# Asking for the compression weights and the second input from ScalarE's queue

## The chip, the cores and the metric

One NeuronCore of one Trainium2 chip runs the whole program. The metric is the device time of one execution in microseconds (us).

## The reference

All arrays are float32; the input x has 256 tokens of width 1024. Two blocks follow each other. The first has two layers (DEPTH = 2), and the change lies in them:

```python
for i in range(DEPTH):
    h = rmsnorm(x, norm_mix[i])
    z = h @ w_in[i]                       # 1024 x 5400
    (q_a, kc, vc, ks_, vs_, kw, vw, g_nsa, rq, rk, rv, rg, merge_a, merge_b) = split_cols(z, IN_SPLITS)
    y_a = nsa_mixer(q_a, kc, vc, ...) @ w_up_nsa[i]
    y_b = retention(rq, rk, rv, rg) @ w_up_ret[i]
    x = x + (sigmoid(merge_a) * y_a + sigmoid(merge_b) * y_b) @ w_out[i]
    x = x + square(relu(rmsnorm(x, norm_mlp[i]) @ w_ff1[i])) @ w_ff2[i]
    gate = sigmoid(rmsnorm(x, norm_ple[i]) @ w_ple_gate[i])
    x = x + gate * (p[i] @ w_ple[i])
```

Inside the mixer, the columns kc and vc of z are compressed: overlapping windows of 32 tokens (plus a learned position term) go through `gelu(zb @ w1) @ w2`, with w1 of 2048 x 256 and w2 of 256 x 64 for keys and the same for values. These are the arrays cmp_w1_k, cmp_w1_v, cmp_w2_k and cmp_w2_v. The array p (2 x 256 x 256) is the second input; it is used only at the end of a layer. The second block (a stick-breaking attention with a state-space model, a sparse attention, two MLPs) is untouched by the change.

## The kernel before

Every large matrix is multiplied in two-digit form: ScalarE copies a weight tile to a rounded high part (`act_split`, line 1053, two halves of 128 x 2048 each), VectorE or GpSimd subtracts it to get the low part (`lower_half`, line 1073, written over the tile in the ring), and TensorE makes three matmuls for each product (line 463).

**The ring.** The weight tiles, 2 MB each (128 x 4096 floats), pass through three SBUF buffers (`RING = 3`). The order is `TILES`: in0 to in10 (512 columns of w_in each), then up_nsa, up_ret, out0, out1, the MLP's and the gate's tiles. Tile n lies in buffer n % 3. SyncE's program (lines 2970 to 3018) walks through TILES, waits until TensorE has used up the tile three places earlier (`tile_used`, line 2998), and issues the tile's load (line 3016). So in4 needs in1's buffer, and in5 needs in2's. SyncE's queue runs in order: whatever it issues between two tiles stands ahead of the second.

**The compression's weights.** Just ahead of in4 (`n == RING + 1`, line 2988), SyncE issues five loads of cmp_w1 (`W1_PARTS`, line 2991: 13 and 3 blocks of the key's matrix, 10, 4 and 2 blocks of the value's; a block is 128 rows of 256 floats, moved in runs of 1 KB; together 4 MB), then the two w2 (line 2994, 64 KB each, runs of 256 bytes) and p (line 2995, 256 KB, runs of 1 KB). They signal `w1_in` (5 x 16) and `late_in` (3 x 16). The parts lie in columns of z that chunks 4 to 10 write later, and in parts of the buffer `work`.

**TensorE in the stretch.** Chunk c computes the 512 columns of tile in{c}, token half 0 and then token half 1 (c{c}t0, c{c}t1), 24 matmuls each, into two PSUM banks used in turn (`wide`). So c2t0 needs the bank of c1t0, and c3t1 the bank of c2t1, to be saved by ScalarE first. After chunk 2 stand four transposes of kc and vc, then chunk 3, then a wait on `w1_in` (line 805) and the compression's matmuls, then transposes that wait for the normalised queries and keys.

**ScalarE in the stretch.** The order is written out by hand in `act_layer`. `save_half(c, t)` (line 1153) copies a bank to z; `act_split` waits for the tile and for the place of its high part:

```python
for c in range(3):
    save_half(c, 0)
    act_split(st, act, TILES, SPLITS, f"in{c + 2}")
    save_half(c, 1)
act.wait_ge(st.last.sem, st.reached())
act.activation(sq, z[:, :, 0:1152], ACT.Square)...
```

So c2t1 is saved only behind in4's split, and the squares of the norm (line 1186) follow it; VectorE then sums them (line 1427), ScalarE takes the root, and VectorE multiplies queries and keys (line 1342). The places of the high parts matter: in3's (`tmp`, `rows`) are in1's, the second of in4's (`work`) is in2's. GpSimd makes the low parts of the in tiles.

Of the kernel before, what the change touches and what calls it, by code (L numbers as in the profile page):

```python
# [14 lines left out]
P = 128  # L15
# [9 lines left out]
RING = 3  # L25
# [5 lines left out]
NCMP, CMP_STRIDE, CMP_LEN, CMP_HID = 16, 16, 32, 256  # L31
# [242 lines left out]
def program(nc, ctx, I, out):  # L274
    address = {}

    def sb(name, shape):
        address[name] = -(-nc.sbuf_base // 32) * 32
        return ctx.enter_context(nc.sbuf_tensor(name, shape, F32))
# [5 lines left out]
    def sig(name, per_layer=0, start=0):  # L285
        return Signal(ctx.enter_context(nc.semaphore(name)), per_layer, start)
# [12 lines left out]
    p_sb = sb("p_sb", [P, TT, PLE])  # L299
# [35 lines left out]
    def part(lo, width, pattern=None, **sizes):  # L335
        ap = work[:, lo:lo + width]
        return ap.rearrange(pattern, **sizes) if pattern else ap
# [9 lines left out]
    W1_PARTS = [(0, 0, 13, z[:, 0, W1_Z:W1_Z + 13 * CMP_HID]), (0, 13, 3, z[:, 1, W1_Z:W1_Z + 3 * CMP_HID]),  # L347
                (1, 0, 10, z[:, 1, W1_Z + 3 * CMP_HID:W1_Z + 13 * CMP_HID]), (1, 10, 4, part(4032, 4 * CMP_HID)),
                (1, 14, 2, part(7264, 2 * CMP_HID))]
# [37 lines left out]
    late_in = sig("late_in", 16 * 3)  # L387
    w1_in, ple_in = sig("w1_in", 16 * len(W1_PARTS)), sig("ple_in", 16)
# [42 lines left out]
    def batch_heads(b):  # L431

        _, h0, nh = BATCHES[b]
        return [4 * g + h for g in range(GROUPS) for h in range(h0, h0 + nh)]
# [10 lines left out]
    def w_tile(n, shape):  # L445

        k, m = shape
        return ring[n % RING][:, 0:k * m].rearrange("p (k n) -> p k n", k=k)
# [583 lines left out]
    def act_norm(st, act, signal=None, power=-0.5, squares=gate_t):  # L1032


        for t in range(TT):
            act.activation(squares[:, t, :], x[:, t, :], ACT.Square, accum_out=nss[:, t:t + 1]).then_inc(st.up(act_step), 1)
        act.wait_ge(st.last.sem, st.reached())
        act_rsqrt(st, act, nrr, nss, 1.0 / D, EPS, signal, power)

    def act_split(st, act, tiles, splits, name, halves=(0, 1)):  # L1040

        n = tiles.index(name)
        act.wait_ge(tile_in[n % RING].sem, st.at(tile_in[n % RING], 16 * (n // RING + 1)))
        places, width = PLACES if splits is SPLITS else PLACES2, split_halves(name)
        for h in halves:

            place = places[name][h]
            earlier = [tiles.index(o) for o in splits[:splits.index(name)] if place in places[o]]
            before = [TILES.index(o) - len(TILES) for o in SPLITS if place in PLACES[o]]
            n_used = (before + earlier)[-1] + 1 + RING if before + earlier else 0  # L1050
            if n_used > 0:
                act.wait_ge(tile_used.sem, st.at(tile_used, n_used))
            act.activation(w_hi[place][:, 0:width], ring[n % RING][:, h * width:(h + 1) * width], ACT.Copy) \  # L1053
                .then_inc(st.up(w_hi_ready), 1)
# [90 lines left out]
    def act_layer(act, st, following):  # L1145
        wide_, aux_ = wide.again(WIDE), aux.again(AUX)

        def save_half(c, t):

            m = min(BANK, D_IN - c * BANK)  # L1150
            b, nth = wide_.next(f"c{c}t{t}")
            act.wait_ge(wide_.ready.sem, st.at(wide_.ready, nth))
            act.activation(z[:, t, c * BANK:c * BANK + m], b[:, 0:m], ACT.Copy, scale=nrr[:, t:t + 1]).then_inc(st.up(wide_.saved), 1)
# [18 lines left out]
        if st.where.layer == 0:  # L1172
            act_norm(st, act)
            act_split(st, act, TILES, SPLITS, "in0")
            act_split(st, act, TILES, SPLITS, "in1")
        else:
            act_split(st, act, TILES, SPLITS, "in1")
            act.wait_ge(ple_added.sem, st.at(ple_added, 0))
            act_norm(st, act)
            act.wait_ge(st.last.sem, st.reached())  # L1180
        for c in range(3):
            save_half(c, 0)
            act_split(st, act, TILES, SPLITS, f"in{c + 2}")
            save_half(c, 1)
        act.wait_ge(st.last.sem, st.reached())
        act.activation(sq, z[:, :, 0:1152], ACT.Square).then_inc(st.up(sq_ready), 1)
        act.wait_ge(ss_ready.sem, st.at(ss_ready, 1))
# [14 lines left out]
        kv, nth = aux_.banks[aux_.names.index("w2") % 2], aux_.names.index("w2") + 1  # L1202
# [19 lines left out]
        b, nth = wide_.next("o0")  # L1222
# [19 lines left out]
        b, nth = wide_.next("o1")  # L1242
# [24 lines left out]
        for n in range(4):  # L1267
            t, half = divmod(n, 2)
# [11 lines left out]
        for n in range(4):  # L1280
            c, t = divmod(n, 2)
            b, nth = wide_.next(f"g{n}")
# [1670 lines left out]
    def small_loads(i):  # L2953

        def vec(name):
            return I[name][i:i + 1]

        small = [(vec_rows[8 * n:8 * n + 8, :], vec(v).rearrange("o (k p) -> (o k) p", p=P))
                 for n, v in enumerate(("norm_mix", "norm_mlp", "norm_ple"))]
        for n, v in ((C_Q, "nsa_q_norm"), (C_K, "nsa_k_norm")):  # L2960
            for u in range(2):
                small.append((vec_rows[n:n + 1, u * DH:(u + 1) * DH], vec(v)))
        for n, v in enumerate(("cmp_pos_k", "cmp_pos_v")):
            small.append((vec_rows[C_POS + 16 * n:C_POS + 16 * n + 16, :],
                          I[v][i].rearrange("(j l) d -> j (l d)", l=2)))
        for n, v in enumerate(("cmp_w2_k", "cmp_w2_v")):
            small.append((w2[:, n], I[v][i].rearrange("(h p) d -> p h d", p=P)))
        return small

    @block.sync  # L2970
    def _(sp):
        sp.dma_start(x[:, :, :], I["x"][0].rearrange("(t p) n -> p t n", p=P)).then_inc(x_in.sem, 16)
        for i in range(DEPTH):
            where = Where(i)

            def src(name):
                return I[name][i]

            if i:
                sp.wait_ge(small_used.sem, i * small_used.per_layer + 1)  # L2980
            small = small_loads(i)
            if i:
                for n, (dst, s) in enumerate(small[:9]):
                    sp.dma_start(dst, s).then_inc((small_in if n else mix_in).sem, 16)
            for n, name in enumerate(TILES):
                if n == RING and i == 0:
                    sp.dma_start(const[:, P:CONST_W], I["const"][:, P:CONST_W]).then_inc(const_in.sem, 16)
                if n == RING + 1:
                    for kind, j0, nj, place in W1_PARTS:
                        s = src("cmp_w1_" + "kv"[kind])[j0 * P:(j0 + nj) * P, :]  # L2990
                        sp.dma_start(place.rearrange("p (j n) -> p j n", n=CMP_HID),  # L2991
                                     s.rearrange("(j p) n -> p j n", p=P)).then_inc(w1_in.sem, 16)
                    for dst, s in small[9:]:
                        sp.dma_start(dst, s).then_inc(late_in.sem, 16)
                    sp.dma_start(p_sb[:, :, :], I["p"][i].rearrange("b s n -> (b s) n")
                                 .rearrange("(t p) n -> p t n", p=P)).then_inc(late_in.sem, 16)

                sp.wait_ge(tile_used.sem, where.value(tile_used, n + 1))
                if name == "ff1.3":
                    sp.dma_start(w_ple, src("w_ple").rearrange("(k p) n -> p k n", p=P)).then_inc(ple_in.sem, 16)  # L3000
                kind, _, num = name.partition(".")
                if name.startswith("in"):
                    c = int(name[2:])
                    m = min(BANK, D_IN - c * BANK)
                    s, k = src("w_in")[:, c * BANK:c * BANK + m], KT
                elif name in ("up_nsa", "up_ret"):
                    s, k, m = src("w_" + name), 4, D
                elif kind == "ff1":
                    s, k, m = src("w_ff1")[:, int(num) * BANK:(int(num) + 1) * BANK], KT, BANK
                elif kind == "ff2":  # L3010
                    s, k, m = src("w_ff2")[int(num) * BANK:(int(num) + 1) * BANK, :], 4, D
                else:
                    c = int(name[-1])
                    s = src("w_out" if name.startswith("out") else "w_ple_gate")[:, c * BANK:(c + 1) * BANK]
                    k, m = KT, BANK
                sp.dma_start(w_tile(n, (k, m)), s.rearrange("(k p) n -> p k n", p=P)) \
                    .then_inc(tile_in[n % RING].sem, 16)
        sp_tail(sp)
# [77 lines left out]
```

## Time and profile before

| | |
|---|---|
| median of 3 runs | 1503.27 us (1499.74 to 1503.67) |
| profiled execution | 1503.03 us, its span 1501.2 us |
| TensorE busy (PE) | 1448.0 us, 96% of the span |
| weight loads (PEld) | 1236.6 us, 82% |
| VectorE (DVE) | 814.0 us, 54% |
| ScalarE (ACT) | 729.6 us, 49% |
| GpSimd (POOL) | 289.2 us, 19% |
| mean granted TensorE clock | 0.993 of full speed |
| DMA | 250.25 MB, mean 167 GB/s |

The engines run side by side, so busy times don't add up. The chain that ended last is followed back from the last instruction to what released each step; its shares tell where the time is set. SPq is SyncE's sequencer with its DMA issues, ACTq is ScalarE's. A DMA issue has a duration of its own, in which the sequencer can do nothing else, and a time to landing. Times in rows are us from the start of the span, unless they are marked as ns. L3016 is line 3016 of the kernel.

### The profile page before, as it was taken

How to read it: one execution, taken by the hardware profiler on the slowest of the kernel's cores; microseconds unless marked ns; L12 is line 12 of the kernel's file. 1: busy time of each engine (PE TensorE's matmuls, PEld its weight loads, DVE VectorE, ACT ScalarE, POOL GpSimd, SP SyncE). 2: the span in 40 equal slices, each digit the busy share in tenths (PEclk: the TensorE clock that was granted, in tenths of full speed). 3: DMA queues.
4: the chain of work that ended last, by engine and by line, in shares of the span. 5: the costliest groups of instructions: out<-in, count | busy, mean ns of one | idle time of the engine just before them, and what ended most of it. 6: DMA issues, size and time to landing. Idle time of an engine off the chain costs nothing.

```text
span 1501.2 us, 19974 instructions
## 1 busy us (share of the span) xinstructions
PE 1448.0 (96%) x8638; PEld 1236.6 (82%) x8638; DVE 814.0 (54%) x1010; ACT 729.6 (49%) x909; POOL 289.2 (19%) x109
## 2 busy tenths in 40 slices
PE   7899999999999999999999989899999999999998
PEld 5688888989877688889989778587988888889986
DVE  5337664444552355754444659876444557654445
ACT  4364635445444563645445346655454326265452
POOL 4589140000027695410000000000000004000000
PEclk9999999999999999999999999999999999999999
DMA  8732435645538432446545362315555453156451
GB/s 309 254 135 89 166 114 200 221 170 200 191 125 302 144 122 98 165 157 230 186 174 205 75 228 99 140 38 187 197 203 189 145 197 113 41 198 236 170 184 69
DMA packets 123142, 250.25 MB, mean 167 GB/s; under 512 B 16960, under 2 KB 28976, under 8 KB 122928
## 3 DMA queue, kind: packets, MB, share of 16 engines
q1 hardware_dynamic: 122792, 248.89, 47.0%
q8 instruction: 68, 1.11, 0.3%
q14 instruction: 18, 0.15, 0.0%
q10 hardware_dynamic: 264, 0.10, 0.0%
HBM read 247.93 MB, written 1.05 MB: 166 GB/s over the span
## 4 chain that ended last, share of the span: by engine, by line
PE 82%; DVE 8%; SPq 5%; DMA 3%; ACT 2%; issue 1%; DVEq 0%; ACTq 0%
PE psum L463 79%; PE psum L470 3%; SPq L2991 2%; DMA ring<-in_w_in 1%; SPq L1817 1%; DVE scr L2499 1%; DVE big L2499 1%; SPq L1810 1%; DMA ring<-in_sb_ssm_w_in 1%; DVE x L2505 1%; DMA ring<-in_w_ff 1%; DVE p_sb L2499 0%; DVE w_lo L1073 0%; DVE rows L2499 0%; DMA work<-in_norm_mix 0%
## 5 line engine op out<-in xcount | busy, mean ns | idle before, releaser
L463 PE MATMUL psum<-ht_hi,w_lo 128*128 128x256 f32 x960 | 270.3, 282 | 7.3 <-issue 3.1
L463 PE MATMUL psum<-w_lo,ht_hi 128*128 128x512 f32 (+1 forms) x576 | 226.0, 392 | 0.0
L463 PE MATMUL psum<-w_lo,hid_hi 128*128 128x512 f32 x512 | 202.4, 395 | 0.0
L463 PEld LDWEIGHTS psum<-ht_hi,w_lo 128*128 128x128 f32 x960 | 180.4, 188 | 10.0 <-issue 8.9
L1053 ACT ACTIVATE w_hi_work<-ring 128x2048 fp32r<-128x2048 f32 x41 | 78.4, 1911 | 150.3 <-PE psum L463 148.8
L1073 DVE TENSOR_TENSOR w_lo<-ring,w_hi_work 128x2048 fp32r<-128x2048 f32 x29 | 66.5, 2292 | 127.2 <-ACT w_hi_work L1053 127.2
L1143 DVE TENSOR_TENSOR hid_lo<-work,hid_hi 128x512 fp32r<-128x512 f32 x60 | 41.5, 692 | 161.9 <-ACT hid_hi L1121 161.9
L463 PEld LDWEIGHTS psum<-w_lo,ht_hi 128*128 128x128 f32 x576 | 109.9, 191 | 21.2 <-issue 1.0
L463 PE MATMUL psum<-ht_lo,w_hi_tmp 128*128 128x256 f32 x448 | 125.6, 280 | 0.0
L463 PE MATMUL psum<-ht_hi,w_hi_tmp 128*128 128x256 f32 x448 | 125.4, 280 | 0.0
L463 PE MATMUL psum<-ht_lo,w_hi_rows 128*128 128x256 f32 x448 | 125.0, 279 | 0.0
L463 PE MATMUL psum<-ht_hi,w_hi_rows 128*128 128x256 f32 x448 | 124.4, 278 | 0.0
L463 PEld LDWEIGHTS psum<-w_lo,hid_hi 128*128 128x128 f32 x512 | 96.1, 188 | 21.7
L1073 DVE TENSOR_TENSOR w_lo<-ring,w_hi_tmp 128x2048 fp32r<-128x2048 f32 x36 | 82.5, 2293 | 46.8 <-ACT w_hi_tmp L1053 46.8
L1073 POOL TENSOR_TENSOR w_lo<-ring,w_hi_work 128x2048 fp32r<-128x2048 f32 x12 | 57.3, 4779 | 260.5 <-ACT w_hi_work L1053 260.5
L1117 ACT ACTIVATE work<-psum 128x512 f32<-128x512 f32 x60 | 35.8, 597 | 144.1 <-PE psum L463 144.1
L463 PE MATMUL psum<-hT,ring 128*128 128x256 f32 (+2 forms) x480 | 91.2, 350 | 6.2 <-DMA ring<-in_sb_ssm_w_in 4.7
L463 PEld LDWEIGHTS psum<-hT,ring 128*128 128x128 f32 (+1 forms) x480 | 79.4, 189 | 17.0 <-issue 7.8
L463 PE MATMUL psum<-w_hi_big,hid_lo 128*128 128x512 f32 x224 | 88.9, 397 | 0.0
L463 PE MATMUL psum<-w_hi_big,hid_hi 128*128 128x512 f32 x224 | 88.4, 395 | 0.0
L463 PE MATMUL psum<-w_hi_work,hid_hi 128*128 128x512 f32 x224 | 88.4, 395 | 0.0
L1053 ACT ACTIVATE w_hi_tmp<-ring 128x2048 fp32r<-128x2048 f32 x42 | 80.0, 1905 | 17.1 <-PE psum L463 10.4
(395 smaller groups left out, 3396.9 us busy)
## 6 DMA issues: line engine op xcount, KB each, us to landing
ring<-in_w_ff SPq DMA_DIRECT2D x32, 2048.0 KB, 7.9
ring<-in_mlp_w SPq DMA_DIRECT2D x32, 2048.0 KB, 8.5
ring<-in_w_in SPq DMA_DIRECT2D x20, 2048.0 KB, 8.4
ring<-in_w_out SPq DMA_DIRECT2D x4, 2048.0 KB, 8.2
ring<-in_w_ple_gate SPq DMA_DIRECT2D x4, 2048.0 KB, 8.0
ring<-in_sb_ssm_w_in SPq DMA_DIRECT2D x4, 2048.0 KB, 10.8
ring<-in_dsa_w_in SPq DMA_DIRECT2D x3, 2048.0 KB, 8.5
ring<-in_w_up_nsa SPq DMA_DIRECT2D x2, 2048.0 KB, 8.5
```

Source lines behind the costliest of these rows:

```text
L463: ins = pe.matmul(o, lhsT, rhs, start=start, stop=stop)
L470: ins = pe.transpose(o, in_, ident[0:n, 0:n])
L1053: act.activation(w_hi[place][:, 0:width], ring[n % RING][:, h * width:(h + 1) * width], ACT.Copy) \
L1073: eng.tensor_tensor(w_lo[n % RING][:, c], ring[n % RING][:, c], w_hi[places[name][h]][:, 0:width].bitcast(F32), ALU.subtract) \
L1117: act.activation(h, b, ACT.Relu).then_inc(st.up(wide_.saved), 1)
L1143: dve.tensor_tensor(lo, h, hi.bitcast(F32), ALU.subtract).then_inc(st.up(hid_lo_ready), 1)
L1810: sp.dma_start(dst, src).then_inc(signal.sem, 16)
L1817: sp.dma_start(dst, src, allow_slow_non_contiguous=True).then_inc(signal.sem, 16)
L2499: return dve.tensor_tensor(o, a, b, op)
L2505: return dve.scalar_tensor_tensor(out=o, in0=a, scalar=s1, in1=b, op0=op0, op1=op1)
L2991: sp.dma_start(place.rearrange("p (j n) -> p j n", n=CMP_HID), s.rearrange("(j p) n -> p j n", p=P)).then_inc(w1_in.sem, 16)
```

## The change

The eight loads leave SyncE's program and are issued by ScalarE, in both layers, behind the save of c0t1 (the end of the first turn of the loop above). Data, destinations and signals stay the same.

```diff
+        def load_compression():
+            i = st.where.layer
+            for kind, j0, nj, place in W1_PARTS:
+                s = I["cmp_w1_" + "kv"[kind]][i][j0 * P:(j0 + nj) * P, :]
+                act.dma_start(place.rearrange("p (j n) -> p j n", n=CMP_HID),
+                              s.rearrange("(j p) n -> p j n", p=P)).then_inc(w1_in.sem, 16)
+            for dst, s in small_loads(i)[9:]:
+                act.dma_start(dst, s).then_inc(late_in.sem, 16)
+            act.dma_start(p_sb[:, :, :], I["p"][i].rearrange("b s n -> (b s) n")
+                          .rearrange("(t p) n -> p t n", p=P)).then_inc(late_in.sem, 16)
+
         for c in range(3):
             save_half(c, 0)
             act_split(st, act, TILES, SPLITS, f"in{c + 2}")
             save_half(c, 1)
+            if c == 0:
+                load_compression()
...
                     sp.dma_start(const[:, P:CONST_W], I["const"][:, P:CONST_W]).then_inc(const_in.sem, 16)
-                if n == RING + 1:
-                    for kind, j0, nj, place in W1_PARTS:
-                        s = src("cmp_w1_" + "kv"[kind])[j0 * P:(j0 + nj) * P, :]
-                        sp.dma_start(place.rearrange("p (j n) -> p j n", n=CMP_HID),
-                                     s.rearrange("(j p) n -> p j n", p=P)).then_inc(w1_in.sem, 16)
-                    for dst, s in small[9:]:
-                        sp.dma_start(dst, s).then_inc(late_in.sem, 16)
-                    sp.dma_start(p_sb[:, :, :], I["p"][i].rearrange("b s n -> (b s) n")
-                                 .rearrange("(t p) n -> p t n", p=P)).then_inc(late_in.sem, 16)
```

## Rows read from the trace of the kernel before

**Rows 1.** The page: TensorE's share of the span, and the chain by engine.
```profile
PE 1448.0 (96%) x8638; PEld 1236.6 (82%) x8638; DVE 814.0 (54%) x1010; ACT 729.6 (49%) x909; POOL 289.2 (19%) x109
...
PE 82%; DVE 8%; SPq 5%; DMA 3%; ACT 2%; issue 1%; DVEq 0%; ACTq 0%
```
**Rows 2.** The chain in order of time, layer 0: start us, us, what.
```profile
29.05 0.37 SPq L3016
...
29.46 0.58 SPq L2991
...
30.08 6.20 SPq L2991
...
42.23 1.42 SPq L2991
...
45.16 0.71 SPq L2995
...
45.91 11.12 DMA ring<-in_w_in
...
60.77 0.58 ACT big L1153
...
75.45 30.01 PE psum L463 x159
```
**Rows 3.** TensorE's timeline: start, us; in brackets idle before and its releaser.
```profile
39.82 0.39 PE L463 MATMUL psum<-w_hi_work,ht_lo 128*128 128x512 f32 x1
...
61.40 0.79 PE L463 MATMUL psum<-w_hi_tmp,ht_lo 128*128 128x512 f32 x1 [4.24 <-ACT big L1153]
...
61.99 0.63 PE L463 MATMUL psum<-w_lo,ht_hi 128*128 128x512 f32 x1
...
69.61 3.00 PE L463 MATMUL psum<-big,work 128*32 128x256 f32 x50
...
471.33 0.39 PE L463 MATMUL psum<-w_hi_work,ht_lo 128*128 128x512 f32 x1
...
491.97 0.50 PE L463 MATMUL psum<-w_hi_tmp,ht_lo 128*128 128x512 f32 x1 [3.30 <-ACT big L1153]
...
499.31 3.00 PE L463 MATMUL psum<-big,work 128*32 128x256 f32 x50
```
**Rows 4.** Windows: length, PE, PEld, DVE, ACT, POOL busy; PEclk, DMA share, GB/s.
```profile
61.40:65.00 3.60, 3.60 (x9) 2.83 (x10) 1.46 (x1) 2.10 (x1) 3.60 (x2) 0.50 0.01 3
```
**Rows 5.** The chain in order of time, layer 1.
```profile
460.79 5.39 SPq L2991
...
476.62 10.98 DMA ring<-in_w_in
```
**Rows 6.** ScalarE's timeline in both layers: saves of c0t1, in3's split.
```profile
32.74 0.66 ACT L1153 ACTIVATE big<-psum,tiny 128x512 f32<-128x512 f32 x1
...
40.31 1.92 ACT L1053 ACTIVATE w_hi_tmp<-ring 128x2048 fp32r<-128x2048 f32 x1 [5.20 <-PE psum L463]
...
463.72 0.67 ACT L1153 ACTIVATE big<-psum,tiny 128x512 f32<-128x512 f32 x1
...
471.82 1.92 ACT L1053 ACTIVATE w_hi_tmp<-ring 128x2048 fp32r<-128x2048 f32 x1 [5.20 <-PE psum L463]
```
**Rows 7.** ScalarE's longest DMA issue at the start: ns min/median/max.
```profile
L3039 ACTq DMA_DIRECT2D work<-in_norm_mix x1: 540/540/540, 1.3 to 1.3; - x1
```
**Rows 8.** Queue's packets, MB, share, in windows 29.05:36.29, 29.05:45.87, 36:37, 51:53.
```profile
q1 hardware_dynamic: 1129, 2.17, 85.4%
...
q1 hardware_dynamic: 4423, 5.52, 99.2%
...
q1 hardware_dynamic: 342, 0.36, 108.9%
...
q1 hardware_dynamic: 378, 0.77, 105.0%
```
**Rows 9.** The same in layer 1, windows 459.75:466.18 and 459.75:473.92.
```profile
q1 hardware_dynamic: 928, 1.90, 83.9%
...
q1 hardware_dynamic: 3515, 4.60, 97.3%
```
**Rows 10.** VectorE's timeline, layer 0: the last of the norm's multiplications.
```profile
69.23 0.75 DVE L1342 TENSOR_TENSOR big<-big,tiny 128x256 f32<-128x256 f32 x2
```

## The prediction

> **What bounds the kernel now.** I read the page first, then the chain that ended last in order of time, then the instruction timelines of SyncE, ScalarE and TensorE around the added and removed lines, then the count of packets that the DMA queue moved. TensorE is busy 96% of the span and the chain lies on it for 82%, but 5% of the chain is SyncE's queue [rows 1]: that is where this change acts, once in each layer. The chain shows the place [rows 2]. SyncE asks for in3 at 29.05, and then spends from 29.46 to 45.87 issuing the five compression parts, the two w2 and p. Only then is in4 asked for, and it lands 11.12 us later, at 57.03. ScalarE has been standing before in4's split; it splits (two halves) and only then saves c2t1 at 60.77. TensorE needs that bank for the second half of chunk 3 and has been idle for 4.24 us [rows 3]. Its clock pays as well: from 61.40 to 65.00 the granted clock is 0.50, the lower of the two levels (1.2 of 2.4 GHz), after the idle stretch, and a matmul lasts 0.63 us against 0.39 [rows 3, 4].
>
> The size of the loss, from the starts of the matmuls [rows 3]: chunk 2 starts at 39.82 and runs gapless with chunk 3's first token to 61.40 - 4.24 = 57.16, so 17.34 us for three halves of 24 matmuls and four short transposes, 5.66 us a half. The last half should end 23.0 us after chunk 2's start; the compression's matmuls start at 69.61, 29.8 us after it. So 6.8 us are lost in layer 0: 4.24 idle and 8.21 - 5.66 = 2.55 for the low clock. In layer 1, 499.31 - 471.33 = 28.0, so 5.0 lost, 3.30 of it idle. The most that the change can give is 11.8 us. The layer 1 issues look the same as in layer 0 [rows 5].
>
> **The change, part by part.** (a) SyncE loses eight issues in each layer, 16.4 us of its queue's time. What keeps in4 back is then its slot: in1 must be used. ScalarE's split of in3 at 40.31 waits for the same event [rows 6], so in4 is asked for at about 40.3 instead of 45.91, and in layer 1 at 471.8 instead of 476.62 (5.6 and 4.8 us earlier, no more).
>
> (b) The eight issues now stand in ScalarE's own stream, behind the save of c0t1, which ends at 33.40 and 464.39 [rows 6]. The question is how long they hold ScalarE. Its nine small issues at the start took at most 0.54 us each [rows 7]; on SyncE the unhindered ones took 0.58 and the others 1.4 to 6.2 [rows 2]. Packet counts explain them [rows 8]. in3 is 1024 packets of 2 KB, the five parts are 1664, 384, 1280, 512 and 256 packets of 1 KB, each w2 is 256. When the last of the eight issues ended (45.87), SyncE had earlier given the queue 5632 packets (through the second w2) and 4423 were moved: 1209 outstanding. In layer 1 the issue of the fifth part ended when 4864 had been given and 3515 moved: 1349 [rows 9]. An issue thus ends when all before it is down to some 1200 to 1350 packets; the first reading of layer 1, 2688 given and 928 moved, would allow 1760 [rows 9]. I assume the same depth for ScalarE's queue, which no row shows.
>
> So ScalarE is free when 4608 - 1209 = 3400 of its packets are moved (layer 1: 4608 - 1349 = 3260). Rates: 342 packets of 1 KB per us, 378/2 = 189 of 2 KB [rows 8]. in3's packets end near 36.0 (1129 moved at 36.29, 105 of them beyond in3), and they began 1.5 us after its issue (1024/189 = 5.4 back from 36.0). Until 36.0 the sharing with in3 only swaps one for the other; from then the parts flow alone until in4's first packets at 40.3 + 1.5 = 41.8: 5.8 x 342 = 1980 moved, 1420 to go. Both loads then share the DMA engines, which one queue alone already fills (108.9% and 105.0%) [rows 8]. How they share, no row shows. With no share for in4: 4.2 us, free at 46.0. By equal bytes: 1420/342 + 710/189 = 7.9, free at 49.7. By equal packets: 1024 pairs take 8.4, the other 396 take 1.2, free at 51.4. I take equal bytes, the middle one. Layer 1: in3's packets end at 466.7, in4's start at 473.3, 2257 moved, 1002 to go; free at 476.2, 478.9 or 481.5.
>
> The Trainium skill, DMA: Bandwidth & Descriptors, section Queues, rings and completion order, says that each DMA engine takes turns between queues by whole packets of descriptors; if these hold equally many descriptors for both loads, that is the third value, and the sum would be +16.4 us. No run here shows two big queues side by side.
>
> (c) What is queued behind ScalarE's issues: the save of c1t0, the split of in3, the save of c1t1. TensorE ends chunk 1 at 39.82 and 471.33 [rows 3] and needs c1t0's bank at once. It therefore stands from 39.82 to 49.7 + 0.69 (one save) = 50.4, where now it stands 4.24 us later on. Then chunk 2 and 3 take their 23.0 us and the low clock its 2.55 once more (the larger of the two layers' values, since this idle is longer). The other work keeps up: in4 has landed by then, the split of in3 (3.8 us) and c1t1's save are done 5 us into chunk 2, c2t1 is saved about 3 us after chunk 2's end, some 3 us before chunk 3's second half. The norm chain, which ends with VectorE's multiplications 9.2 us after c2t1's save (60.77 to 69.98) [rows 2, 10], is done before the compression's matmuls end. in5 and in6 are asked for later, by the same amount as TensorE. The compression weights have landed before 56, some 20 us before they are used. All this costs nothing while that holds; without that cover the first thing late would be the norm chain, by 1 to 3 us.
>
> (d) The sum. The compression's matmuls start at free + 0.69 + 23.0 + 2.55 = free + 26.2. Layer 0: 75.9 against 69.61, +6.3. Layer 1: 505.1 against 499.31, +5.8. TensorE is gapless for 30 us from 75.45 on [rows 2], so the delay reaches the end. Total +12.1 us on an execution of 1503.03 us (span 1501.2), whose time is 0.2 below the median of the runs, too little to correct: **1515.1 us**. Bounds: no share for in4 and 1760 outstanding give free at 44.3 and 475.0, +0.9 and +1.9, total +2.8, 1506; equal packets give +8.0 and +8.4, total +16.4, 1519.5.
>
> **Rivals.**
> Faster: ScalarE's queue takes the eight without blocking, 0.62 us each as the first one on SyncE, and is free at 38.4, before TensorE needs c1t0. in4 shares with the parts from 41.8, at worst 8.4 us, lands near 52, and c2t1 is saved before 57.2. The whole 6.8 + 5.0 = 11.8 us come back: 1491.3. For it: the part's bytes are few and ScalarE's queue is empty. Against it: every run of such issues on SyncE blocked as soon as a thousand packets were ahead [rows 2, 5]. Chance 0.12.
> The Trainium skill, same page, section Issuing engines are not separate DMA queues, says that issuing from several engines saves the sequencer's issue time, which is usually small beside the DMA; by that rule this rival wins. The trace disagrees for this load: the issues took 16.4 us.
>
> About the same: the queue holds more than SyncE's seemed to, or the descriptors of in4 are made only after those of the parts, so that ScalarE is free near 44. The break-even is free = 43.4 and 473.1. It gives 1503 to 1508, and in it one wait of 4 us is swapped for another. For it: layer 1's first reading. Against it: the last reading of each layer, 1209 and 1349. Chance 0.10.
>
> The forecast, ScalarE blocked to about 50 and 479: chance 0.78, of which 0.05 lies above 1521 (in3's split or the norm chain late as well). That the change does nothing is excluded but for the small gain in (a).
>
> **Numbers.** 0.3% is 4.5 us, about what a measurement of this kernel can tell from no change. Faster 0.12, within 0.10, slower 0.78. The range must leave out at most 0.2: the faster case and the uppermost tail, so it runs from 1503 to 1521. The forecast's own range is 1506 to 1520.
>
> **What would show it.** In the profile after: the eight issues on ScalarE's queue, ending near 50 and 479, the middle ones 2 to 6 us long; TensorE idle about 10 and 7.5 us at the start of chunk 2, released by ScalarE's save; no wait before chunk 3's second half; in4 asked for near 40.3; the granted clock at 0.5 behind the new idle. Eight short issues would make me wrong, and so would an end of ScalarE's issues before 44: then the depth or the sharing of the queues was misread. If the issues end where I say and the time still does not grow, the step (d) is wrong.

## The result, and the profile after

The changed kernel takes 1507.56 us (median of 13 runs, 1504.64 to 1509.01) against 1503.27 us (1499.74 to 1504.95, 13 runs): ratio 1.0029, interval 1.0021 to 1.0036, so 3.2 to 5.4 us more. Two later measurements gave 1.0022 (1.0011 to 1.0033) and 1.0035 (1.0015 to 1.0054). The profiled execution took 1504.64 us, span 1502.8, the fastest of the 13; executions of one kernel differ by 4 to 5 us, so below I compare stretches of a few tens of us and not whole spans.

The page of the changed kernel: the shares, SyncE's queue gone down on the chain from 5% to 2%, and a second queue (q10, ScalarE's) that now moves 9.27 MB (0.10 before).

```profile
PE 1447.0 (96%) x8638; PEld 1235.5 (82%) x8638; DVE 812.3 (54%) x1010; ACT 729.8 (49%) x909; POOL 289.3 (19%) x109
...
q10 hardware_dynamic: 10248, 9.27, 2.0%
...
PE 85%; DVE 8%; SPq 2%; issue 2%; DMA 1%; ACT 1%; POOL 1%; DVEq 0%; ACTq 0%
```

ScalarE's timeline in layer 0, changed kernel (start, us; idle before in brackets). It answers to [rows 2, 6].

```profile
29.61 4.94 ACTq L1185 DMA_DIRECT2D big<-in_cmp_w_k  x2
...
33.17 0.66 ACT L1153 ACTIVATE big<-psum,tiny 128x512 f32<-128x512 f32 x1
34.58 2.91 ACTq L1185 DMA_DIRECT2D big<-in_cmp_w_v  x1
37.52 5.95 ACTq L1185 DMA_DIRECT2D work<-in_cmp_w_v  x2
43.50 0.60 ACTq L1188 DMA_DIRECT2D work<-in_cmp_w_k  x1
44.12 1.17 ACTq L1188 DMA_DIRECT2D work<-in_cmp_w_v  x1
45.33 0.72 ACTq L1189 DMA_DIRECT2D p_sb<-in_p  x1
46.10 0.69 ACT L1153 ACTIVATE big<-psum,tiny 128x512 f32<-128x512 f32 x1 [12.27 <-issue]
```

Two things are to be seen. The issues do hold ScalarE: the save of c1t0, whose bank was full by about 34.4 in the kernel before, is made at 46.10. And they begin at 29.61, though the save of c0t1, which stands ahead of them in the program, runs only at 33.17: the sequencer passed the copies on to the engine and went ahead to the next issue, since every wait that stands between was met by then. The depth of the queue can be read too. When the last issue ended (46.05, and 475.01 in layer 1), ScalarE had earlier given its queue 4608 packets, and 3273 and 2965 of them were moved (windows 29:46.05 and 459:475.01): 1335 and 1643 outstanding, where the prediction took 1209 and 1349 from SyncE's queue.

TensorE's timeline, both layers, changed kernel, which answers to [rows 3]:

```profile
46.88 0.77 PE L463 MATMUL psum<-w_hi_work,ht_lo 128*128 128x512 f32 x1 [6.47 <-issue]
...
71.57 3.00 PE L463 MATMUL psum<-big,work 128*32 128x256 f32 x50
...
475.85 0.77 PE L463 MATMUL psum<-w_hi_work,ht_lo 128*128 128x512 f32 x1 [4.69 <-issue]
...
501.06 3.00 PE L463 MATMUL psum<-big,work 128*32 128x256 f32 x50
```

The wait has changed places: 4.24 us before chunk 3's second half are gone, and 6.47 us stand before chunk 2; in layer 1 it is 3.30 against 4.69. From the end of chunk 1 to the compression's matmuls it was 69.61 - 39.82 = 29.79 and 27.98 us; it is 71.57 - 40.41 = 31.16 and 501.06 - 471.16 = 29.90. That is 1.4 and 1.9 us more, 3.3 together, the lower end of what the runs show. (I count from chunk 1's end because the two traces also drift by some 2 us between the two layers.) The clock pays in the new place as it did in the old one. Windows of the changed kernel (length, PE, PEld, DVE, ACT, POOL busy, granted clock, DMA share, GB/s), the first the idle stretch, the second the first nine matmuls behind it:

```profile
40.41:46.88 6.47, 0.00 (x1) 0.03 (x1) 0.00 (x0) 0.69 (x1) 0.29 (x1) 0.77 1.09 348
...
46.88:50.80 3.92, 3.92 (x9) 3.12 (x10) 0.00 (x0) 3.05 (x2) 1.06 (x1) 0.51 1.12 336
```

Last, in4's load. It should have been asked for at 40.3; SyncE asked at 47.68 (changed kernel, SyncE's timeline), and ScalarE's split of in4, which waits for its landing, starts at 56.99, where it started at 57.06 before. TensorE now needs what hangs on it later, so no second wait arises:

```profile
47.68 0.37 SPq L3020 DMA_DIRECT2D ring<-in_w_in  x1
...
56.99 1.92 ACT L1053 ACTIVATE w_hi_hT<-ring 128x2048 fp32r<-128x2048 f32 x1 [1.81 <-DMA ring<-in_w_in]
```

The program says why. A used tile is not given back by its own last matmul (that one signals the full bank) but by the next instruction of TensorE that has no signal of its own (`pay` in `mm`, called by `tile_done`'s debt). Behind chunk 1 that is chunk 2's first matmul, and this one waits for ScalarE's save of c1t0. So ScalarE's block held back in4's request too.

### The profile page after: what moved, and what is told of

Same layout as the page of the kernel before. It is cut to its first block, busy times and chain, and to the rows that moved or that the text cites. A ratio compares the mean times of both kernels' runs of the same rounds, so it can differ in the third digit from the quotient of the medians.

```text
span 1502.8 us, 19974 instructions
## 1 busy us (share of the span) xinstructions
PE 1447.0 (96%) x8638; PEld 1235.5 (82%) x8638; DVE 812.3 (54%) x1010; ACT 729.8 (49%) x909; POOL 289.3 (19%) x109
## 3 DMA queue, kind: packets, MB, share of 16 engines
q10 hardware_dynamic: 10248, 9.27, 2.0%
## 4 chain that ended last, share of the span: by engine, by line
PE 85%; DVE 8%; SPq 2%; issue 2%; DMA 1%; ACT 1%; POOL 1%; DVEq 0%; ACTq 0%
PE psum L463 82%; PE psum L470 3%; SPq L1830 1%; DVE scr L2512 1%; DVE big L2512 1%; SPq L1823 1%; DMA ring<-in_sb_ssm_w_in 1%; DVE x L2518 1%; POOL w_lo L1073 1%; DVE p_sb L2512 0%; DVE rows L2512 0%; DMA work<-in_norm_mix 0%; DVE rows L1355 0%; DVE pT L2762 0%; DVE p_sb L2518 0%
## 5 line engine op out<-in xcount | busy, mean ns | idle before, releaser
L463 PE MATMUL psum<-w_hi_work,hid_lo 128*128 128x512 f32 x224 | 88.2, 394 | 0.0
## 6 DMA issues: line engine op xcount, KB each, us to landing
ring<-in_sb_ssm_w_in SPq DMA_DIRECT2D x4, 2048.0 KB, 11.3
```

The costliest lines, as they stand in the source:

```text
L463: ins = pe.matmul(o, lhsT, rhs, start=start, stop=stop)
```

## The experiments

Two theories stood after this. A: ScalarE's blocked issues stall TensorE, and the stall holds back in4; the block's length is the bytes that in3 and the parts have to move. B: something of the queues themselves (the order in which the hardware takes them, or the traffic) sets the time, whoever issues. Each expectation below puts its own A and B, narrowed to what the run can tell apart. The edits of the runs from e5_release to e3_three are shown against the changed kernel, that of e4_sp_behind against the kernel before.

**in1 given back early (e5_release).** The changed kernel and one instruction more on TensorE:

```diff
         for c in range(1, 3):
             chunk(c)
+            if c == 1:
+                tp(scores[:, 3 * BANK:3 * BANK + P], ident)
```

> The changed kernel, with one transpose of the identity (into an unused PSUM bank) behind chunk 1, so that in1 is given back by it and no longer by chunk 2's first matmul. Theory A (in4 came late in the changed kernel because in1's release hangs on a matmul that itself waits for ScalarE; the two queues share by equal packets, 122 against 122 per us while in3 and the parts overlapped): in4 is asked for near 40.5 and 471.3, its packets start 1.5 us later beside the parts, ScalarE's last issue ends near 51.5 instead of 46.05 and near 478.8 instead of 475.01, TensorE starts chunk 2 5.4 and 3.8 us later, total 1507.6 + 9.2 = 1516.8 us. Theory B (the queue makes in4's descriptors only behind ScalarE's): in4 is asked for early but its packets start only near 49.5 as in the changed kernel, ScalarE is free at 46, total 1507.6 us.

Measured: 1515.36 us, ratio 1.0084 (1.0066 to 1.0101). This is the situation that the prediction assumed, in4 asked for early, and the time is the 1515.1 forecast for it (1516.8 was expected of this run). ScalarE's and TensorE's timelines of this kernel, layer 0, and SyncE's request of in4:

```profile
40.14 0.37 SPq L3022 DMA_DIRECT2D ring<-in_w_in  x1
...
44.94 4.68 ACTq L1190 DMA_DIRECT2D work<-in_cmp_w_v  x1
49.65 0.67 ACTq L1191 DMA_DIRECT2D p_sb<-in_p  x1
...
51.16 0.77 PE L463 MATMUL psum<-w_hi_work,ht_lo 128*128 128x512 f32 x1 [11.05 <-issue]
```

The issues end at 50.3 and TensorE waits 11.05 us; in layer 1 it waits 7.98. TensorE's waits are 4.6 and 3.3 us longer than in the changed kernel, where 5.4 and 3.8 were expected. From chunk 1's end to the compression's matmuls: 76.59 - 40.11 = 36.5 and 509.92 - 476.36 = 33.6 us, 5.3 and 3.7 more; behind the longer wait the low clock costs more as well (2.4 and 2.6 us beyond the undisturbed 23.0, where the changed kernel has 1.7 and 2.2). The DMA queues of this kernel in the windows 43:44, 44:45, 46:47 and 48:49 (packets, MB, share of 16 engines; q1 is SyncE's, q10 ScalarE's):

```profile
q10 hardware_dynamic: 344, 0.35, 110.0%
...
q10 hardware_dynamic: 177, 0.18, 55.6%
q1 hardware_dynamic: 89, 0.18, 52.5%
...
q1 hardware_dynamic: 119, 0.24, 68.4%
q10 hardware_dynamic: 124, 0.13, 36.8%
...
q1 hardware_dynamic: 124, 0.25, 70.8%
q10 hardware_dynamic: 124, 0.12, 35.2%
```

The queues share packet by packet: 124 of 2 KB against 124 of 1 KB. That is what the Trainium skill says (DMA: Bandwidth & Descriptors, Queues, rings and completion order: each engine takes turns between queues by packets); the trace agrees for packets as it counts them. Theory B has a small part of the truth: in4's first packets came at 44.2, some 4.1 us behind the issue and not 1.5, after 1411 packets of ScalarE's queue had moved in between.

**The start of the issues (e6_wait).** ScalarE waits for its save before it issues:

```diff
             if c == 0:
+                act.wait_ge(st.last.sem, st.reached())
                 load_compression()
```

> The changed kernel, with ScalarE waiting until the save of c0t1 is done before it issues the eight loads. Theory A (the end of the issues is set by the bytes that in3 and the parts move together, since one queue alone fills the engines): the issues start near 33.9 instead of 29.6, and their end stays at 46 to 46.5, total 1507 to 1509 us. Theory B (the end moves with the start): the end at 50.3, TensorE's wait 4.2 us longer in each layer, total 1516 us.

Measured: 1506.29 us, ratio 1.0021 (1.0011 to 1.0031), as the changed kernel on that chip. The first and the last issue of this kernel:

```profile
34.52 2.71 ACTq L1185 DMA_DIRECT2D big<-in_cmp_w_k  x2
...
46.20 0.72 ACTq L1189 DMA_DIRECT2D p_sb<-in_p  x1
```

They start 4.4 us behind in3's request (30.13) instead of 0.1, and end 16.8 us behind it against 16.6 in the changed kernel (46.05 - 29.47). Theory A holds: the end is set by what must be moved, not by the start.

**Three issues less on ScalarE (e2_five).** The two w2 and p go back to SyncE, ahead of in4; `load_compression` (renamed `load_parts`) keeps only the five parts.

```diff
...
-            for dst, s in small_loads(i)[9:]:
-                act.dma_start(dst, s).then_inc(late_in.sem, 16)
-            act.dma_start(p_sb[:, :, :], ...).then_inc(late_in.sem, 16)
...
+                if n == RING + 1:
+                    for dst, s in small[9:]:
+                        sp.dma_start(dst, s).then_inc(late_in.sem, 16)
+                    sp.dma_start(p_sb[:, :, :], ...).then_inc(late_in.sem, 16)
```

> The changed kernel with the two w2 and p back on SyncE's queue ahead of in4; only the five parts stay on ScalarE's. Theory A (each issue on ScalarE holds TensorE until it ends): the fifth part's issue ended at 43.47 and 472.80 in the changed kernel, 2.6 and 2.2 us before the eighth; SyncE's 768 small packets now share with the parts, which costs back some 1 to 2 us a layer; total 1503 to 1506 us, wait at chunk 2 some 4 to 5.5 and 2.5 to 4 us. Theory B (the slowdown is in4's late landing, not ScalarE's block): in4 lands when it did, total 1507.6 us.

Measured: 1504.63 us, ratio 1.0011 (1.0002 to 1.0020). The waits at chunk 2 were 5.9 and 3.7 us, the first above the 4 to 5.5 expected: the fifth part's issue ended at 45.28, not 43.47, since the moved packets share with the parts (236 of SyncE's queue beside 232 of ScalarE's in the window 40:41). The size fits A; B's 1507.6 lies at the edge of what these runs can exclude, and it is the waits that decide.

**The changed kernel twice more (after_again, e7_again).**

> The changed kernel once more, for the spread between profiled executions. Theory A: the compression's matmuls start 1.5 to 2.5 us later than before in layer 0 and again 1.5 to 2.5 us in layer 1, median 1506 to 1509. Theory B (the 4.3 us are spread over stages that the change does not touch): layer 0 and 1 give less than 1 us each and the difference shows up behind 505 us.

> The changed kernel beside the versions above on the same chip, for a ratio with a narrow interval. Theory A: waits of 6.5 and 4.7 us at chunk 2's start, 1506 to 1508 us, 0.2 to 0.35% over the kernel before.

Measured: 1506.04 and 1506.91 us (ratios above). The waits at chunk 2's start were 6.76 and 4.8 us, and 6.74 us in layer 0 of the other. From chunk 1's end to the compression's matmuls the first took 72.63 - 40.97 = 31.66 and 502.88 - 473.34 = 29.54 us, 1.9 and 1.6 more than before; the other took 1.9 and 2.1 more. With the first profile that makes 3.3, 3.4 and 4.0 us in the two layers, against medians of 4.3, 2.7 and 4.0 us: within the spread, the whole loss lies in these stretches. The profiled execution of after_again has also some 3 us more behind layer 1 than the first profile of the changed kernel, in stages that the change does not touch: that is the spread between executions.

**The issues spread over three chunks (e1_spread).** `load_parts` and `load_late` are `load_compression` cut in two.

```diff
...
             if c == 0:
-                load_compression()
+                load_parts(W1_PARTS[:3])
+            if c == 1:
+                load_parts(W1_PARTS[3:])
+            if c == 2:
+                load_late()
```

> All eight loads on ScalarE's queue, but spread: the first three parts behind chunk 0's saves, the last two behind chunk 1's, the two w2 and p behind chunk 2's. Theory A (the change lost only because the later issues, kept waiting by a full queue, stood ahead of the save of c1t0): the third part's issue ends at 37.5 before chunk 1 does (39.8), so no wait at chunk 2's start; in4 is asked for near 40.2 and shares by equal packets, its packets end at 50.2 to 52.8, so there is no wait or up to 1.7 us before chunk 3's second half. The 6.8 and 5.0 us come back: 1491.5 to 1495 us. Theory B (the DMA traffic itself is the bound of this stretch, whoever asks): in4 lands near 57 as in both kernels, and the time is 1503 us.

Measured: 1494.52 us, ratio 0.9936 (0.9922 to 0.9949). ScalarE's timeline:

```profile
34.21 3.13 ACTq L1185 DMA_DIRECT2D big<-in_cmp_w_v  x1
37.39 0.69 ACT L1153 ACTIVATE big<-psum,tiny 128x512 f32<-128x512 f32 x1 [3.88 <-issue]
...
40.70 4.67 ACTq L1185 DMA_DIRECT2D work<-in_cmp_w_v  x2
...
53.70 1.92 ACT L1053 ACTIVATE w_hi_hT<-ring 128x2048 fp32r<-128x2048 f32 x1 [7.31 <-DMA ring<-in_w_in]
```

ScalarE is still held, to 37.34, but nobody needs it before 39.9, and chunk 2 starts without a wait. in4, asked for at 40.35, shares with the parts and lands 13.3 us later; 0.8 and 1.3 us of waiting are left before chunk 3's second half.

**Three parts on ScalarE, the rest on SyncE (e3_three).**

```diff
...
             if c == 0:
-                load_compression()
+                load_parts(W1_PARTS[:3])
...
+                if n == RING + 1:
+                    for kind, j0, nj, place in W1_PARTS[3:]:
...
+                    for dst, s in small[9:]:
...
+                    sp.dma_start(p_sb[:, :, :], ...).then_inc(late_in.sem, 16)
```

> The first three parts on ScalarE's queue behind c0t1's save, the last two, the two w2 and p on SyncE's queue ahead of in4. Theory A (both count: ScalarE's block, and in4's place in its queue): ScalarE is free at 37.5, so no wait at chunk 2's start, but in4 is asked for behind 1536 packets of its own queue that share packet by packet with ScalarE's; it lands near 57 and the wait of 4 to 5 us before chunk 3's second half is back; total 1503 us. Theory B (only ScalarE's block counts): in4 lands in time, 1491.5 us.

Measured: 1502.33 us, ratio 1.0002 (0.9990 to 1.0014). No wait at chunk 2, and the old one is back. This kernel's chain and TensorE's timeline:

```profile
40.83 16.61 DMA ring<-in_w_in
...
61.81 0.79 PE L463 MATMUL psum<-w_hi_tmp,ht_lo 128*128 128x512 f32 x1 [4.05 <-ACT big L1153]
```

in4 is asked for at 40.83 and lands 16.6 us later, behind its own queue's packets and sharing with ScalarE's. An early request gains nothing if the bytes ahead of it stay.

**All on SyncE, but behind in4 (e4_sp_behind).** The kernel before with one character changed:

```diff
-                if n == RING + 1:
+                if n == RING + 2:
```

> The kernel before, with the same eight issues on SyncE moved by one tile, from ahead of in4 to behind it. Theory A (in4's late landing cost the kernel before 6.8 and 5.0 us): in4 is asked for at 40.2, alone on the engines, and lands at 48.6; the parts follow, the last lands near 60.5, before the compression's matmuls can start at 62.8; 1491.5 us, or up to 1494 if the parts are late by a microsecond or so. Theory B (the parts become what is late, since the engines have idled from 36 to 41.8): they land at 65 or later and the time is 1496 to 1500 us.

Measured: 1491.95 us, ratio 0.9923 (0.9910 to 0.9936), the fastest of all. SyncE's, ScalarE's and TensorE's timelines:

```profile
41.70 5.30 SPq L2991 DMA_DIRECT2D big<-in_cmp_w_k  x2
47.04 2.31 SPq L2991 DMA_DIRECT2D big<-in_cmp_w_v  x1
...
56.09 0.71 SPq L2995 DMA_DIRECT2D p_sb<-in_p  x1
...
49.14 1.92 ACT L1053 ACTIVATE w_hi_hT<-ring 128x2048 fp32r<-128x2048 f32 x1 [1.80 <-DMA ring<-in_w_in]
...
63.75 3.00 PE L463 MATMUL psum<-big,work 128*32 128x256 f32 x50
```

SyncE is blocked about as long as before (41.70 to 56.80), and nothing urgent is behind it: only in5's request, made at 56.85, some 4.5 us after its buffer came free, and no wait of TensorE follows from that. in4 lands at 49.1, neither wait is left, and from chunk 1's end to the compression's matmuls it takes 63.75 - 40.87 = 22.9 us (layer 1: 22.9), the 23.0 of the prediction's undisturbed count. The parts are not late either.

## Why the prediction was right or wrong

**Right: what bounded the kernel and the size of the loss.** 6.8 and 5.0 us, 11.8 together, were to be had; e4_sp_behind took 1502.96 - 1491.95 = 11.0 of them, with both waits gone.

**Right: the direction, the wait that takes the place of the old one, and its mechanism.** ScalarE's issues block it, the depth seen on SyncE's queue holds roughly for ScalarE's too (1335 and 1643 packets for 1209 and 1349), and TensorE waits at chunk 2's start for the save of c1t0. The faster rival, eight short issues, did not happen.

**Wrong: the size, +12.1 us against +4.3.** The step that failed is in (a) and (b): in4 was to be asked for at 40.3 and to prolong ScalarE's block from 46.0 to 49.7. It was asked for at 47.68, when ScalarE was free. I had taken the event "in1 is used" from the split of in3 [rows 6] and treated it as fixed in time, while in the code it is counted by chunk 2's first matmul, which the predicted stall itself delays. With in4 out of the way the issues ended at 46.05 and 475.01, close to the "no share" values of 46.0 and 476.2 that stood in the same paragraph; counted from in3's request (29.47 and 459.40; 29.05 and 459.75 before) they ended 0.4 and 0.8 us sooner than those, and the 126 and 294 packets more that were outstanding are worth just that at 342 per us.

Put into the sum of step (d), counted from chunk 1's end as the traces are shifted, the measured block gives (46.05 - 40.41) + 26.2 - 29.79 = 2.1 and (475.01 - 471.16) + 26.2 - 27.98 = 2.1, 4.1 us in all, where the medians of the three measurements say 4.3, 2.7 and 4.0. So the rest of the mechanism was sound. Of the 8 us by which the forecast was too high, in4's share in the block was 49.7 - 46.0 and 478.9 - 476.2, 6.4 in all.

e5_release, which takes that hold away, ran at 1515.4, beside the 1515.1 of the forecast. That it is so close is partly luck, as two errors cancel: the share was by equal packets, not by bytes, which prolongs the block, and in4's packets started 4.1 us behind the request and not 1.5, which shortens it.

The rival "about the same" had the right time, 1503 to 1508, and the right picture of one wait swapped for another, with a chance of 0.10. Both its reasons exist in small (a deeper queue; in4's packets 4.1 us late in e5_release), but e5_release has them too and took 1515.4: what held the time down was that in4 was not asked for.

**Off, without weight.** The start of the issues: I put them behind the save's end (33.40), they began at 29.61; e6_wait shows that it does not matter. The low clock: 2.55 us assumed for both layers. Chunk 2 took 13.15 and 13.64 us against 11.3 undisturbed (17.34 less the 5.66 of a half and the transposes' 0.36), 1.8 and 2.3 us. The reading that all hindered issues took 1.4 to 6.2 us: in the kernel before, the last three (two w2 and p) took 0.67 to 0.71 us each with the queue as full (p's is the row at 45.16 in [rows 2]). Each followed a load of 256 packets, 0.75 us at 342 per us.

**The check that I gave for myself** said that the issues would end near 50 and 479, with waits of about 10 and 7.5 us; they ended at 46.05 and 475.01 with 6.5 and 4.7. The trace before could have told this: it was enough to ask which instruction signals `tile_used`, and whether that instruction waits for the engine that is about to be blocked.

## What to carry to other kernels

Before a DMA issue is moved to a compute engine, count the packets ahead of it in the queue: in these runs an issue ended only when those given earlier were down to some 1050 to 1760, and whatever was written behind it waited. First ask whether the load only stands in the wrong place of the order: here moving it behind the urgent tile on the same idle queue gave 11 us, and moving it to another engine cost 4. And when a stall is forecast, follow which signals its own victims were to give, since requests hung on them move too.

## What the runs showed of the hardware

Two queues that both have work share the DMA engines by equal numbers of packets (124 and 124 in one us), not by bytes, so that the queue with 2 KB packets gets two thirds; one queue alone moved 342 packets of 1 KB [rows 8] or 190 of 2 KB per us (changed kernel, window 52:53).

An issue ended when the packets given earlier on that queue were down to 1335 and 1643 on ScalarE's queue in the changed kernel, 1238 in layer 0 of e6_wait, and 1053 and 1163 in e5_release, beside in4's packets (counts in the windows 28.5:46.92, 29:50.32 and 461:483.50).

A load issued on one queue while the other had that many packets to go sent its first packets some 4.1 us later instead of 1.5, three times: e5_release, 40.14 to 44.2 and 476.39 to 480.45, and e1_spread, 40.35 to 44.4. In between 1411, 1404 and 1407 packets of the other queue moved. In e1_spread no issue of ScalarE was running at 40.35, so an issue in progress is not what it takes. That the load lines up behind packets already prepared would fit; no run tries it.

ScalarE's sequencer issued its first DMA at 29.61, while the copies that stand ahead of it in its program ran until 33.83; every wait between was met by then. With a wait for the last copy put in (e6_wait) the first issue came at 34.52.
